# Two transformer blocks on one core: a projection moved between two latent stages, a gate moved ahead of the last transposes, and shorter first steps of two attentions

## What is computed

```
z = h @ w_in
z_cq, z_ckv, z_kr, z_sq, z_sk, z_sv, z_gate = split_cols(z, EVEN_SPLITS)   # 384, 256, 32, 512, 128, 128, 1024
q  = (rmsnorm(z_cq,  q_norm)  @ w_uq )    # 8 heads x (64 + 32 with rope)
kv = (rmsnorm(z_ckv, kv_norm) @ w_ukv)    # 8 heads x (64 keys + 64 values)
o_mla = mla_attention(q_nope, q_rope, k_nope, k_rope, v_mla)          # causal softmax
q_s = apply_rope(z_sq); k_s = apply_rope(z_sk); v_s = z_sv
o_swa = swa_sink_attention(q_s, k_s, v_s, sinks)                      # window of 128, a sink per head
o = concatenate([o_mla, o_swa]) * silu(z_gate)
y = o @ w_out
```

## Time and profile before

| what | value |
|---|---|
| median of three runs | 1381.34 us |
| the profiled execution | 1383.62 us |
| its span, first to last instruction | 1381.8 us |
| TensorE busy | 1223.5 us (89%) |
| share of TensorE in the chain that ended last | 75% |
| VectorE, ScalarE busy | 552.5 us (40%), 427.6 us (31%) |
| mean granted TensorE clock | 0.925 |

### The profile page before, as it was taken

One profiled execution on the slowest core, in us unless ns is written; L12 is line 12 of the kernel. 1 busy time (PEld: TensorE's weight loads), 2 busy tenths in 40 slices (PEclk: granted clock), 3 DMA queues, 4 the chain that ended last, 5 costly groups with the idle time before them and its releaser, 6 DMA issues.

```text
span 1381.8 us, 15110 instructions
## 1 busy us (share of the span) xinstructions
PE 1223.5 (89%) x5264; PEld 684.8 (50%) x5264; DVE 552.5 (40%) x1422; ACT 427.6 (31%) x1086; POOL 112.5 (8%) x140
## 2 busy tenths in 40 slices
PE   4879989999898899979999989989999899867974
PEld 1555454455564444334455555555454556445541
DVE  3234323333544320334443432112225632758871
ACT  0133013444451101222234321114344544651211
POOL 0000000000002000000000000000000000574722
PEclk8889989999998999999999999999999999856997
DMA  9321234463002422332111005241101111000000
GB/s 347 105 92 31 93 127 177 160 226 73 0 1 70 77 38 61 70 111 61 62 61 61 1 11 137 62 167 46 46 1 46 46 62 62 1 3 30 1 32 30
DMA packets 60258, 99.71 MB, mean 72 GB/s; under 512 B 12068, under 2 KB 22129, under 8 KB 60184
## 3 DMA queue, kind: packets, MB, share of 16 engines
q1 hardware_dynamic: 54370, 93.58, 21.9%
q10 hardware_dynamic: 5814, 5.18, 1.2%
HBM read 96.60 MB, written 4.08 MB: 73 GB/s over the span
## 4 chain that ended last, share of the span: by engine, by line
PE 75%; DVE 13%; ACT 6%; issue 2%; DMA 2%; ACTq 1%; POOL 0%; DVEq 0%; SPq 0%; POOLq 0%
PE PR L867 33%; PE OB L897 6%; PE PT L779 6%; PE SC L919 6%; PE PR L779 5%; PE OB L779 4%; PE SC L779 4%; PE PT L934 3%; PE PR L960 3%; DVE stage L1677 2%; DMA ring<-in_w_ada 2%; DVE d L1677 1%; DVE tok L1677 1%; DVE arena L1893 1%; PE PT L867 1%
## 5 line engine op out<-in xcount | busy, mean ns | idle before, releaser
L867 PE MATMUL PR<-ring,hT 128*128 128x512 f32 (+1 forms) x784 | 381.7, 600 | 4.8 <-ACT hT L1208 4.0
L867 PEld LDWEIGHTS PR<-ring,hT 128*128 128x128 f32 x784 | 137.7, 199 | 105.0 <-issue 87.8
L1367 ACT ACTIVATE stage<-stage,nmax 128x256 f32<-128x256 f32 (+7 forms) x200 | 103.7, 519 | 264.7 <-DVE nmax L2023 233.5
L897 PEld LDWEIGHTS OB<-arena,pts 128*128 128x128 f32 (+3 forms) x880 | 133.1, 202 | 99.9 <-issue 76.8
L867 PE MATMUL PR<-hT,ring 128*128 128x512 f32 (+1 forms) x304 | 149.9, 616 | 0.0
L1585 POOL TENSOR_TENSOR arena<-arena 128x192 f32<-128x192 f32 (+1 forms) x118 | 80.1, 679 | 798.3 <-PE OB L897 749.5
L897 PE MATMUL OB<-arena,pts 128*128 128x64 f32 (+4 forms) x880 | 131.4, 279 | 11.5 <-ACT pts L1208 11.5
L919 PE MATMUL SC<-arena 64*128 64x256 f32 (+15 forms) x432 | 114.9, 459 | 10.2 <-DVE nmax L2023 10.2
L934 PEld LDWEIGHTS PT<-ident,stage 128*128 128x128 f32 (+3 forms) x440 | 59.1, 147 | 110.7 <-issue 69.0
L934 PE MATMUL PT<-ident,stage 128*128 128x128 f32 (+3 forms) x440 | 87.2, 290 | 24.6 <-ACT stage L1339 11.8
L1208 ACT ACTIVATE pts<-PT 128x256 f32<-128x256 f32 (+7 forms) x200 | 80.9, 404 | 84.0 <-PE PT L934 62.4
(11 more groups left out here) (337 smaller groups left out, 1288.5 us busy)
## 6 DMA issues: line engine op xcount, KB each, us to landing
ring<-in_w_ada SPq DMA_DIRECT2D x12, 2048.0 KB, 8.3
ring<-in_od_w_in SPq DMA_DIRECT2D x8, 2048.0 KB, 16.7
ring<-in_w_in SPq DMA_DIRECT2D x5, 1536.0 KB, 6.9
ring<-in_ev_w_in SPq DMA_DIRECT2D x3, 2048.0 KB, 7.7
ring<-in_w_in SPq DMA_DIRECT2D x3, 2048.0 KB, 10.0
ring<-in_ev_w_out SPq DMA_DIRECT2D x2, 2048.0 KB, 10.2
ring<-in_od_w_out SPq DMA_DIRECT2D x2, 2048.0 KB, 8.0
ring<-in_w_out SPq DMA_DIRECT2D x2, 2048.0 KB, 7.7
```

Of the source, the lines that this page charges most:

```text
L867: mm = pe.matmul(dst, l, r, start=(k == 0), stop=(k == KT - 1))
L897: mm = pe.matmul(ob[:, h * w:h * w + w], pts[0:rows_, v % 2, n * P:n * P + P], vb, start=(n == 0), stop=(n == len(blocks) - 1))
L1367: give(act.activation(pb[:, s % NP, 0:n], zm[:, s % 2, 0:n], ACT.Exp, bias=nmax[:, row, c:c + 1], scale=-1.0, accum_out=rsum[:, row, c:c + ...
```

## The change

Three parts.

1. `sq` moves. TensorE now does: relation rows, `sq` 0, the four `cqT`, `sq` 1, the four `ckvT`, `sqT` 0, `sq` 2, `sqT` 1, `sq` 3, `sqT` 2; then `uq` 0, `sqT` 3, and `uq` and `ukv` as before. Its roped queries go to `tok[:, 0, :]` instead of `stage`. The chunk `sq` is loaded ahead of `uq`. VectorE's and ScalarE's lists are reordered to match.
2. The gate's first tile stands ahead of `skT` 3, and the chunk `skv` ends with `skT` 2.
3. The first step of the attentions of layer 1 and of the second block issues scores up to `need + 1`: two instead of three and four.

```diff
@@ pr_plan
-    transposes("cqT")
-    transposes("ckvT")
+    chunk(("w", "sq"), [("sq", 0)] + [("cqT", i) for i in range(T)] + [("sq", 1)] + [("ckvT", i) for i in range(T)]
+          + [("sqT", 0), ("sq", 2), ("sqT", 1), ("sq", 3), ("sqT", 2)])
     for w, t in (("uq", "mqT"), ("ukv", "mkT")):
         u = []
         for i in range(T + 1):
             if i < T:
                 u += [(w, i, 0), (w, i, 1)]
+            if (w, i) == ("uq", 0):
+                u.append(("sqT", T - 1))
...
-    chunk(("w", "sq"), with_transposes("sq", "sqT"))
-    chunk(("w", "skv"), with_transposes("skv", "skT"))
+    chunk(("w", "skv"), with_transposes("skv", "skT")[:-1])
     jobs.append(("gate0", 0, 0))
+    jobs.append(("skT", T - 1))
@@ two_block_kernel
+        sqtok = tok[:, 0, :].rearrange("p (b n) -> p b n", b=2)
@@ steps
-                upto = min(need + LOOK, s_all[-1])
+                upto = min(need + (1 if v == mine[0] and L != 1 else LOOK), s_all[-1])
@@ tensor
+            W = weights(("w", "sq"))
+
+            def swa_transposes(i):
+                drained(pe, ("sq", i))
+                transposes(("sqT", i), [sqtok[:, i % 2, k * P:k * P + P] for k in range(4)])
+
+            token_major(("sq", 0), W, 0, 0, 512)
             for i in range(T):
                 if i == 0:
                     drained(pe, ("ckv", T - 1))
                 transposes(("cqT", i), [cqn[:, i, k * P:k * P + P] for k in range(3)])
+            token_major(("sq", 1), W, 1, 0, 512)
             for i in range(T):
                 transposes(("ckvT", i), [ckvn[:, i, k * P:k * P + P] for k in range(2)])
+            for i in range(T - 1):
+                swa_transposes(i)
+                if i + 2 < T:
+                    token_major(("sq", i + 2), W, i + 2, 0, 512)
...
+                    if (w, i) == ("uq", 0):
+                        swa_transposes(T - 1)
@@ roped
+                    if i == T and name[0] == "skv":
+                        whole_tile(("gate0", 0, 0))
                     if i >= 1:
                         drained(pe, (name[0], i - 1))
...
-            roped(("sq", "sqT"), 512, 4, rtok)
             roped(("skv", "skT"), 256, 1, rktok)
-            whole_tile(("gate0", 0, 0))
-            banks_back(pe, ("gate0", 0, 0))
+            banks_back(pe, ("skT", T - 1))
```

More of the change, by code:

```diff
@@ L189, in pr_plan @@
     chunk_end = {}
-    def transposes(name):
-        jobs.extend((name, i) for i in range(T))
     def last_tile(L):
@@ L1464, in _ @@
             for i in range(T):
+                b = take(act, ("sqT", i))
+                release(copy(a0["sqT"][:, :, i * P:i * P + P], heads(b[:, :])), ("sqT", i))
+            for i in range(T):
                 for g in range(2):
@@ L1477, in _ @@
                     release(copy(mv, b[:, :, MN:2 * MN]), ("ukv", i, g))
-            for i in range(T):
-                b = take(act, ("sqT", i))
-                release(copy(a0["sqT"][:, :, i * P:i * P + P], heads(b[:, :])), ("sqT", i))
             for i in range(T):
@@ L2113, in _ @@
                 if i >= 2:
+                    used(dve, ("sqT", i - 2))
+                b = take(dve, ("sq", i))[:, :].rearrange("p (n w) -> p n w", n=NH)
+                u, w = rope(None, b, NH, MN, cosh_[:, i, :], sinh_[:, i, :])
+                dst = sqtok[:, i % 2, :].rearrange("p (j v d) -> p v j d", j=4, v=2)
+                four = lambda z: z.rearrange("p (v j) d -> p v j d", v=2)
+                for kv in range(2):
+                    ins = tt(dst[:, kv, :, :], four(u)[:, kv, :, :], four(w)[:, kv, :, :], ALU.add)
+                    if kv == 0:
+                        link(ins)
+                release(ins, ("sq", i))
+            for i in range(T):
+                if i >= 2:
                     used(dve, ("mqT", i - 2, 1))
@@ L2125, in _ @@
                                             b[0:MQ, :].rearrange("p (j t) -> p j t", j=4)), ("mkT", i, g))
[L2126 to L2138, removed]
             for i in range(T):
```

## The result

Four executions of the changed kernel have a median of 1367.47 us (1365.13 to 1374.62) against 1382.66 us of before; the ratio is 0.9894 (95% interval 0.9845 to 0.9943), 14.6 us off 1382.66. The experiments timed it again in five more sets. All 35 executions together have a mean of 1369.9 us (1358.9 to 1377.3), the 118 of the kernel before 1382.4 us (1377.0 to 1389.9): 12.5 us, a third less than the 18.4 that were forecast. The median of the first four lies inside the range that was forecast, the mean of the 35 above it.

What follows compares the result with a forecast made beforehand. TensorE was taken to bound the kernel, busy in 89% of the span, with its waits and the low clock behind them. Gains summed to 18.4 us, 1381.34 - 18.4 = 1363.0 us; range 1357.5 to 1368.

Steps and rivals of the forecast that it cites:

- Terms (a) to (d): Moving `sq`: 9.39 us of time ahead of `uq`, 2.63 `uq` warm, 2.45 `sqT` 3's wait, 1.69 `skv` 0 warm.
- part 2's 0.17: At the gate: `skT` 3 leaves the path and falls into the wait for the first masked score, 0.17 us gained.
- The covers: SP's weight loads: `uq` and `ukv` over 20 us before use, the gate's 15.9 us against 12.5 needed.
- fill the wait: Gate ahead of `skT` 3: expected not to fill the 1.54 us rope wait, since its bank holds `skv` 3.
- So I take the low values: Two scores in first steps: low clock assumed behind idles of 2.9 and 3.0 us; gains 1.3 and 0.7 us.
- nothing gained, 0: Lower bound for two scores in attentions 1 and 3: 0 us if weights come late or the wait moves.
- The bound from above: Heads of attentions 1 and 3: if the clock stays up, 2.9 and 3.2 us of slow stretch go too.
- the low end of the range: 1357.5 us: heads of attentions 1 and 3 both warm, 2.9 + 2.5 = 5.4 us more, 1357.6.
- a little for later stages: Allowance at the range's high end, 1368 us, above 1367.3 for the clock falling at both remaining places.
- part 3 brings nothing, 1365.0: Rival: two scores in the first steps gain nothing, strip weights late or the wait moved; 1365.0 us, chance 0.07.
- The rival on the clock: Clock falls at waits that stay, `mqT` 3, `mkT` 3 or the gate: 1364.7 to 1367.3 us, chance 0.15.
- its thought on later stages: Shifting the code by 16 us may deal slow matmuls anew in all later stages; no size given.

Runs made afterwards that it cites:

- part 1 alone: The kernel before with only the move of `sq`, gate behind `skT` 3 and three scores as before: ratio 0.9892, median 1369.21 us.
- fifth trace: The changed kernel as it is, profiled a fifth time: span 1371.4 us; ratio of its set to the kernel before 0.9892.
- the version with the other bank: The changed kernel with the second bank counter started at 1, so the gate's tile gets PR1: ratio 0.9874 to the kernel before.
- with thrown-away matmuls: Changed kernel, bank counter at 1, all fillers ahead, one result-discarded matmul in attention 1's and two in attention 3's first wait: 0.984, median 1361.82 us.

## Why the prediction was wrong

**Part 1: right, by its mechanism and its size.** Terms (a) to (d) with part 2's 0.17 made 16.4 us; the gate starts 16.33 us earlier in the first pair of traces, and 16.0 us earlier over ten, counted from the end of the opening; part 1 alone has 15.8 of its 16.2. `uq` and `skv` start at the high level, `sqT` 3 doesn't wait, no load is late. The covers held: SP's loads of `sq`, `uq` and `ukv` show no wait.

**Part 2: right that it doesn't fill the wait.** The bank was the reason, shown by starting the counter at 1. Its own 0.17 us isn't there (heads of 120.4 without it, 120.3 with it): `skT` 3 and its copy didn't fall into the wait behind the first scores, they hold the scores back.

**Part 3: wrong, and this is the step that failed.** "So I take the low values", 1.3 and 0.7 us, counted the matmuls moved into an idle and took the low clock behind it as a fixed sum. Alone it brings nothing (1.0021, 0.9998 to 1.0043). In attention 1 the transpose did come 2 us earlier, as forecast (the idle ahead of it is 2.37 us, not 2.9), but the low stretch then lies over more work: gate to the fourth step takes 24.9 us (197.48 less 172.58) against 24.96 before, where the clock is low for 6.8 us in both; where the low stretch is shorter, 23.4 (fifth trace) against 23.85 (part 1 alone). That is 0.1 to 0.4 us, and 0.5 by the means of ten traces, where 1.3 stood. In attention 3 the first transpose too stands where it was forecast, 4.13 us behind the first score (before 5.56), and yet it is a gain of 0.1 us on one course and on the other a loss of 3.6, 3.5 and 0.1 in three traces. The bound of "nothing gained, 0" was too kind: a gain was bounded from above by a clock that stays up, but a loss by a clock that stays down longer wasn't thought of. The bound from above was too large as well: 1.3 and 2.9 make 4.2 us in attention 1, and the version with the other bank, with no low stretch there, gains 3.1 (24.9 to 21.8), since the 1.3 was counted at the low level; the low end of the range rests on it. The working itself could have told: it leaves idles of 2.9 and 3.0 us where there were 3.58 and 2.99, so in attention 3 nothing would change ahead of the low stretch, and nothing said that it would end as early as before once other work lay under it.

**The range.** 1357.5 to 1368 misses 1369.9. The base, one median of three, was 1.1 us below the mean of 118. Of the 5.9 us between 18.4 and 12.5, the ten traces put 0.4 ahead of the gate, 0.8 in attention 1 (0.5 for 1.3) and 1.9 in attention 3 (a loss of 1.2 for a gain of 0.7); the rest, some 2.8 us, isn't located, and its cause stays open. It isn't part 3's: part 1 alone and the version without part 3, which issue three and four scores, are 15.0 and 12.1 us faster by the means of their own sets, 13.5 together, give or take 2, where the sum has 16.2 and 16.4 for them and their traces show the gate 15.8 and 16.0 us earlier. So something seems to be given back in stages whose code is the same. That is the second step that failed: the sum had no term for it, only "a little for later stages" in the range. It may be scatter in part: 35 executions of the changed kernel have a standard deviation of 4.4 us, 118 of before 2.8. Why the changed kernel scatters more stays open. By its mechanism the rival "part 3 brings nothing, 1365.0", with 0.07, was nearest. The rival on the clock priced `mqT` 3, `mkT` 3 and the gate, which no low stretch follows in any of the six traces; its thought on later stages was the right one and had no price. Also, one execution's trace was taken to stand for all: its agreement with the sum to 0.1 us was a chance, since the traces of the changed kernel lie from 1360.5 to 1373.9.

**A version that beats both.** Bank counter at 1 and all fillers ahead in the first steps: 0.9847, with thrown-away matmuls 0.984, that is 21 to 22 us off 1382.4 and about 9 off the changed kernel's mean of 1369.9 (6.8 off its mean in the same set). The thrown-away matmuls add nothing that the intervals show.

## What to carry to other kernels

A stall is worth its own length plus what the clock does behind it, and the second part is a draw: price it from several traces of one kernel, and bound it on both sides. Moving work into an idle paid here where what was left of the idle was short: 1.2 and 1.5 us with the clock up behind it where all of the work was moved, and 2.4 us with the clock down behind it in all six traces of the changed kernel, where half was. Between these it is open: 2.4 us in attention 1 and 2.25 in attention 3 each had the clock up behind them in one trace of another version. And before work is put ahead of a wait, look at which buffer it gets: a tile that takes the bank of the very result that is waited for doesn't pass it.

## What the runs showed of the hardware

- Behind one and the same idle of 2.37 us the granted clock fell for the strip's second half in the six traces of the changed kernel (1.57 to 1.94 us) and not in that with the other bank (1.06 us). Behind 2.25 us in attention 3 it stayed up in one trace and was low in another (1.00 and 0.57). The opposite also stands in the rows: 3.58 us of wait with the fall at once (third score 0.80 us) and with the fall only behind the next 8 records (0.49 us).
- The courses repeat: where the 12 us ahead of attention 3 have 0.86, its part takes 171.5 to 171.7 us in nine traces, with two scores or four. Where they have 0.72, it takes 172.4 in all three traces with four scores, and 172.5, 175.9 and 176.0 with two (the versions with all fillers ahead left aside). Its first 400 records there take 107.1 with four and 110.1 or 110.2 with two.
- The 35 executions of the changed kernel lie within 18 us, the 118 of before within 13, and the medians of sets of four to ten of the 35 lie up to 2.5 us beside their mean.
